# Two hybrid decoder layers on one core: attention work of both token groups moved by half a slab to four slabs, and one load moved six slabs earlier

## The chip, the cores and the metric

The kernel runs on one core of one Trainium2 chip. The metric is the device time of one execution in microseconds (us). Before the change the median of three runs is 2673.43 us (2672.96 to 2676.93). Trainium2's engines, as the profile calls them: PE (TensorE, matrix products), DVE (VectorE), ACT (ScalarE), POOL (GpSimd), SP (SyncE, which here only issues loads). Each runs its own list of instructions in the order written and waits on semaphores for the others.

## The reference

1056 token rows of width 1024 (a prompt of 1024 and 8 sample sequences of 4 rows) go through two layers, each a mixer and a ConvFFN. What matters here is the second layer's mixer D (attention over keys that an indexer picks) and its mixer C (pooling):

```python
def index_select(qi, wi, ki_all, pos_q, k_sel):
    dots = jax.nn.relu(jnp.einsum('nthd,nsd->nths', qi, ki_all))
    score = jnp.einsum('nth,nths->nts', wi, dots).astype(jnp.float32)
    admissible = jnp.arange(ki_all.shape[1])[None, :] <= pos_q[:, None]
    score = jnp.where(admissible[None], score, -jnp.inf)
    _, idx = lax.top_k(score, k_sel)      # 256 of the prompt's, 129 of a sample's 516
    return idx

def sparse_attend(q, ks, vs, idx, pos_q):
    logits = jnp.einsum('nthd,ntkhd->nthk', q, ks).astype(jnp.float32) * ATT_SCALE
    valid = (idx <= pos_q[None, :, None])[:, :, None, :]
    p = jax.nn.softmax(jnp.where(valid, logits, -jnp.inf), axis=-1).astype(q.dtype)
    return jnp.einsum('nthk,ntkhd->nthd', p, vs)

def odd_mixer(x, pool_hist, pos, attn_fn, w_in, c_w, c_scale, w_out):
    ...
    pooled = multiscale_pool(ext, pos).reshape(n, t, C_GROUPS, C_GROUP_W)
    c_out = jnp.einsum('ntgc,gcd->ntgd', pooled, c_w).reshape(n, t, C_W) * c_scale
    att = attn_fn(q, k, v, qi, ki, wi).reshape(n, t, ATT_W)
    y = jnp.concatenate([c_out, att], axis=-1) @ w_out
    return y, ext[:, -POOL_HIST:], k, v, ki

def conv_ffn(x, hist, w_up, conv_w, conv_b, w_down):
    hu = x @ w_up
    ext = jnp.concatenate([hist, hu], axis=1)
    hc = causal_dwconv(ext, conv_w) + conv_b
    y = (jax.nn.silu(hc[..., :D_FF]) * hc[..., D_FF:]) @ w_down
    return y, ext[:, -(CONV_W - 1):]
```

## The kernel before

**Slabs.** All large products are cut into 400 slabs, one weight block of 128 output columns each, numbered n in time. The tokens are in two groups: GA (the first 512 prompt rows) and GB (the other 512 and the 32 sample rows). A slab of depth 8 is 24 matmuls of 512 columns for GA and 48 of 272 for GB: each weight is split into a high part WH (copied by ACT, L1096) and a rest WL (subtracted by POOL, L1580), each input into XH and XL, and three products are added. SP loads the weights (RAW, L611) into a ring of three buffers, so the load of slab n waits until slab n-3 is multiplied. Products go to two pairs of PSUM banks in turn, so slab n also waits until slab n-2 is emptied (by ACT in up projections, by DVE, tile Z, in down projections).

**Stages that matter.** GB's first ConvFFN covers n = 150 to 209 (`F0C` to `O1A`); GA's second ConvFFN covers n = 240 to 315 (`F1A` to `O1B`), then comes GB's output projection from n = 316 (`O1B`). A ConvFFN is four blocks: 2*nb up slabs and then 8 down slabs, nb = 4, 6, 6, 6. Below, "slab +k" is slab F1A+k; +0 to +7, +16 to +27, +36 to +47 and +56 to +67 are up, the others down. In an up slab ACT empties the banks (extA or extB, cvA or cvB), DVE adds two convolution taps (L1877, L1879) and after each pair of slabs multiplies the halves; ACT and DVE split the hidden chunk (HHA, HLA). At the end of each block PE waits for the last chunk's HLA (or HL).

**Work beside the slabs.** Every engine calls `beside(n, end)` twice per slab: end = 0 in PE's middle of a slab (before ACT and DVE empty it), end = 1 after it. This is where attention runs, and fixed tables of n decide what is called where:

- Prompt attention: `units_at(n, end)` gives for each of 16 pairs of heads the half slab of each step. GA's pairs begin every 6 half slabs (`A_FIRST`, `A_PERIOD`) beside GB's first ConvFFN, GB's every 4 (`B_FIRST`, `B_PERIOD`) from slab +37. The steps are logits (PE, L927), row maximum (DVE), exp (ACT, L1353), reciprocal (DVE, L2343), scaling of the probabilities (ACT, tile PRA or PRB, L1357), turning them (PE, L941, into one PSUM bank), copying the turned ones (ACT, PTA or PTB, L1369), the product with the values (PE, L956), copy (ACT, L1378) and rest (DVE, L2349).
- GB's search: DVE's `best` units (MAX8 and MATCH_REPLACE8 on SC, L2215 and L2213) find the 256 best of blocks 4 and 5; `TOP45` says how many stand in each slab. Blocks 6 and 7 are found by bisection: `threshold` (small DVE operations on tk, one step for each `STEPS67` entry from +10) and `signs_of` (ACT, L1303, two sign passes per step) wait for each other, and `threshold` stands last in DVE's beside.
- Sample search: 16 `sample_round`s (MAX8 and MATCH_REPLACE8 on ssc, L2183 and L2185) and a `sample_bias`, all DVE.
- Sample attention: `sample_at(n)` and `kept_at(n)`, counted from F1A + `S_FIRST`: eight slabs with the logits of one sequence each (PE, L871), then eight with its values (PE, L892 and L895), with a softmax for each four sequences, PE's L904 and ACT's copies of the result (atts, L1340) at a = 12 and 16. Pages of keys and values are loaded by SP two sequences ahead.
- Mixer C of GB: the pooled rows lie in DRAM; ACT issues the load into pooledB and of cw1 (L1443, L1444), which lie over the searches' scores and biases; `c_mixed` (PE, L976), `c_kept` (ACT, L1385) and `c_rest` (DVE, L2356) follow the last slab of GA's ConvFFN, and groups 2 and 3 of `c_mixed` wait for `c_rest` of groups 0 and 1.

Of the kernel before, what the change touches and what calls it, by code (L numbers as in the profile page):

```python
# [106 lines left out]
def centred_rows(q, n, lag=0):  # L107
# [9 lines left out]
DOTS67 = 1  # L117
S_DOTS, S_FIRST = 4, 16
B_FIRST, B_PERIOD = 74, 4
TOPA = dict(zip(range(I1A + 16, F0C + 26), [2] * 32))  # L120
TOP45 = dict(zip(list(range(F1A + 2, F1A + 7)) + list(range(F1A + 16, F1A + 42)),
                 [3, 3, 2, 2, 2] + [4] * 12 + [5] * 8 + [4, 5, 5, 5, 5, 4]))
BEST = TOPK_P // 8
TOPS = (2, 3), (4,), (5,)
assert sum(TOPA.values()) == 2 * BEST and sum(TOP45.values()) == 4 * BEST

# [12 lines left out]
def units_at(n, end):  # L139


    if F0C <= n < O1A:
        p, first, begins = 2 * (n - F0C) + end, 0, [A_FIRST + A_PERIOD * r for r in range(16)]
    elif F1A <= n < O1B:
        p, first = 2 * (n - F1A) + end, 32
        begins = [B_FIRST + B_PERIOD * r for r in range(16)]
    else:
        return [[]] * 9

    def pair(lag):  # L150
        return [first + 2 * r + x for r in range(16) if begins[r] == p - lag for x in range(2)]

    return [pair(0), pair(1), pair(2), pair(3), pair(4), pair(5)[:1] + pair(6)[1:], pair(7), pair(7), pair(8)]

# [44 lines left out]
def build(nc, io):  # L199
    with ExitStack() as ctx:  # L200
# [248 lines left out]
        def pair(p, n, rows=P):  # L449

            return PS[0:rows, 2 * p:2 * p + 2, :].rearrange("p b t -> p (b t)")[:, 0:n]
# [635 lines left out]
        def _(act):  # L1087
# [299 lines left out]
            def beside(n, end):  # L1387
# [47 lines left out]
                if n == F1A + 55 and end:  # L1435
# [3 lines left out]
                    act.dma_start(Z[:, :, COL[GB]], xb_rows).then_inc(zb_in, 16)  # L1439
                if n == O1B - 1 and end:  # L1440
                    act.wait_ge(lg, 64)
                    act.wait_ge(atp, 64)
                    act.dma_start(pooledB[:, :, :], pooled_rows).then_inc(pooled_in, 16)  # L1443
                    act.dma_start(cw1[:, :, :], io["cw"]).then_inc(cw_in, 16)  # L1444
# [341 lines left out]
        def _(dve):  # L1786
# [571 lines left out]

            taken = [0]

            def beside(n, end):
# [23 lines left out]
                if (n, end) == (F1A + S_DOTS + 4, 0):  # L2385
                    blocked(lambda half, h: QBs[h // 2][half, :].rearrange("p (s r) -> p s r", s=SEQS)[
                        :, :, DEC * (h % 2):DEC * (h % 2) + DEC], QB_, qb_zero, 4, qb_set)
                r = 2 * (n - F1A - S_DOTS - 3)
                if end and 0 <= r < TOPK_S // 8:
                    sample_round(r)  # L2390
                    sample_round(r + 1)
                if (n, end) == (F1A + S_DOTS + 11, 0):
                    sample_bias()
# [190 lines left out]
```

## Time and profile before

| | before |
|---|---|
| median of three runs | 2673.43 us (2672.96 to 2676.93) |
| the profiled execution | 2667.54 us |
| its span, first to last instruction | 2665.8 us |
| PE busy | 2501.6 us, 94% |
| DVE, ACT, POOL busy | 1481.5, 1214.0, 1459.8 us |
| mean granted TensorE clock | 0.973 of full speed |

PE is busy in nearly all of the span, so what a change can give is in the 6% in which it is not, and in which work takes PE's place. The profiled execution is 5.9 us under the median; terms below are worked out against it.

### The profile page before, as it was taken

Reading aid. Unit: us, or ns where it says so; the run is one execution under the profiler, and the core shown is the slowest. Engines: PE = TensorE matmul, PEld = TensorE weight load, DVE = VectorE, ACT = ScalarE, POOL = GpSimd, SP = SyncE. Lnnn points to the kernel's source line nnn. Section 1 sums busy time; section 2 is a strip of 40 time slices with the busy share of each in tenths; the row PEclk is TensorE's granted clock in tenths of the full one; section 3 lists DMA queues with packets and bytes.
Section 4 is the critical chain, followed back from the end, with each engine's and each line's share of the span. In section 5 each row is a group of like instructions: output and inputs, shape, how many; then the busy total and the mean of one; then the engine's idle time right before and its main releaser. Section 6 shows DMA issues by size and latency. Waiting matters only on the chain.

```text
span 2665.8 us, 40768 instructions
## 1 busy us (share of the span) xinstructions
PE 2501.6 (94%) x15830; PEld 2198.1 (82%) x15830; DVE 1481.5 (56%) x2335; ACT 1214.0 (46%) x1958; POOL 1459.8 (55%) x2070
## 2 busy tenths in 40 slices
PE   8999999999999999999999987897799988999997
PEld 8999887888888788988989864666577777999997
DVE  2333576343575587643567458987954546452345
ACT  3211364343443434454543455675696725332333
POOL 3322677565676954444478777333334446655554
PEclk9999999999999999999999998999899998999998
DMA  3111222223323221222234321563113122223222
GB/s 139 41 41 49 88 90 91 95 91 99 95 64 117 80 81 65 78 66 78 66 101 143 96 91 61 184 188 95 40 56 103 56 92 95 86 76 100 84 90 82
DMA packets 97068, 235.51 MB, mean 88 GB/s; under 512 B 11434, under 2 KB 32458, under 8 KB 96490
## 3 DMA queue, kind: packets, MB, share of 16 engines
q1 hardware_dynamic: 85344, 210.95, 25.0%
q10 hardware_dynamic: 11530, 21.94, 2.3%
q8 instruction: 126, 2.06, 0.3%
q14 instruction: 68, 0.56, 0.1%
HBM read 219.40 MB, written 13.45 MB: 87 GB/s over the span
## 4 chain that ended last, share of the span: by engine, by line
PE 31%; DVE 12%; ACT 3%; POOL 3%; issue 2%; DMA 1%; ACTq 0%; DVEq 0%; POOLq 0%
PE PS L676 9%; PE PS L677 9%; PE PS L680 9%; DVE SC L2213 2%; DVE m8a L2215 2%; POOL WL L1580 1%; PE PS L956 1%; DVE cvA L1879 1%; PE PS L941 1%; PE PS L927 1%; PE PS L850 1%; DVE cvA L1877 1%; ACT signs L1303 0%; DVE ssc L2185 0%; POOL SC L1639 0%
## 5 line engine op out<-in xcount | busy, mean ns | idle before, releaser
L1580 POOL TENSOR_TENSOR WL<-RAW,WH 128x256 fp32r<-128x256 f32 x1440 | 1149.4, 829 | 1140.9 <-ACT WH L1096 1140.5
L676 PE MATMUL PS<-XH,WH 128*128 128x272 f32 (+2 forms) x3312 | 1059.2, 330 | 33.8 <-DVE XL L1976 9.9
L677 PE MATMUL PS<-XL,WH 128*128 128x272 f32 (+2 forms) x3312 | 1042.8, 326 | 0.0
L680 PE MATMUL PS<-XH,WL 128*128 128x272 f32 (+2 forms) x3312 | 873.1, 325 | 1.8 <-POOL WL L1580 1.8
L676 PEld LDWEIGHTS PS<-XH,WH 128*128 128x128 f32 x3312 | 628.3, 190 | 107.1 <-issue 56.6
L1096 ACT ACTIVATE WH<-RAW 128x1024 fp32r<-128x1024 f32 (+2 forms) x400 | 388.3, 971 | 635.8 <-DMA RAW<-in_slabs 609.8
L677 PEld LDWEIGHTS PS<-XL,WH 128*128 128x128 f32 x3312 | 628.5, 190 | 40.1 <-issue 1.0
L680 PEld LDWEIGHTS PS<-XH,WL 128*128 128x128 f32 x3312 | 559.1, 189 | 44.5 <-POOL WL L1580 2.4
L676 PE MATMUL PS<-HH,WH 128*128 128x272 f32 (+1 forms) x880 | 262.4, 313 | 13.1 <-DVE HL L1997 13.0
L677 PE MATMUL PS<-HL,WH 128*128 128x272 f32 (+1 forms) x880 | 260.2, 310 | 0.0
L680 PE MATMUL PS<-HH,WL 128*128 128x272 f32 (+1 forms) x880 | 215.7, 310 | 0.0
L1870 DVE TENSOR_SCALAR cvB<-extB,fpar 128x560 f32<-128x560 f32 x88 | 55.9, 635 | 254.4 <-POOL extB L1700 210.2
L1877 DVE SCALAR_TENSOR_TENSOR cvB<-extB,fpar,cvB 128x560 f32<-128x560 f32 (+1 forms) x132 | 118.0, 894 | 134.4 <-ACT cvB L1247 131.3
L676 PEld LDWEIGHTS PS<-HH,WH 128*128 128x128 f32 x880 | 167.0, 190 | 25.8 <-DVE HL L1997 14.1
L1924 DVE TENSOR_TENSOR Z<-Z,PS 128x512 f32<-128x512 f32 (+1 forms) x96 | 67.6, 704 | 213.4 <-PE PS L680 212.4
L677 PEld LDWEIGHTS PS<-HL,WH 128*128 128x128 f32 x880 | 166.9, 190 | 7.9
L1244 ACT ACTIVATE extB<-PS 128x240 f32<-128x240 f32 (+3 forms) x308 | 92.2, 363 | 161.0 <-PE PS L680 161.0
L680 PEld LDWEIGHTS PS<-HH,WL 128*128 128x128 f32 x880 | 145.0, 189 | 7.3
L1879 DVE SCALAR_TENSOR_TENSOR cvB<-extB,fpar,cvB 128x560 f32<-128x560 f32 (+1 forms) x132 | 116.4, 882 | 4.7
L1625 POOL TENSOR_TENSOR Z<-Z,sqb 128x512 f32<-128x512 f32 (+1 forms) x64 | 96.3, 1522 | 13.0 <-ACT sqb L1173 13.0
L676 PE MATMUL PS<-HHA,WH 128*128 128x512 f32 x176 | 76.9, 437 | 24.2 <-DVE HLA L1997 12.1
L1303 ACT ACTIVATE signs<-SC,tk 128x896 int8<-128x896 f32 (+1 forms) x62 | 73.1, 1181 | 49.1 <-DVEq L2318 49.1
(335 smaller groups left out, 3139.7 us busy)
## 6 DMA issues: line engine op xcount, KB each, us to landing
RAW<-in_slabs SPq DMA_DIRECT2D x272, 512.0 KB, 3.7
RAW<-in_slabs SPq DMA_DIRECT2D x96, 384.0 KB, 3.1
RAW<-in_slabs SPq DMA_DIRECT2D x32, 256.0 KB, 2.7
KP<-in_ck SPq DMA_DIRECT2D x16, 256.0 KB, 3.5
VP<-in_ck SPq DMA_DIRECT2D x16, 256.0 KB, 3.4
KP<-in_cv SPq DMA_DIRECT2D x16, 256.0 KB, 3.1
VP<-in_cv SPq DMA_DIRECT2D x16, 256.0 KB, 3.0
xb_rows<-spill ACTq DMA_DIRECT2D x8, 272.0 KB, 2.4
```

Of the source, the lines that this page charges most:

```text
L676: pe.matmul(o, WH[n % 3][:, k, :], hi(k)[:, c], start=first, stop=False)
L677: pe.matmul(o, WH[n % 3][:, k, :], lo(k)[:, c], start=False, stop=False)
L680: mm = pe.matmul(o, WL[n % 3][:, k, :], hi(k)[:, c], start=False, stop=last)
L1096: act.activation(WH[n % 3][:, 0:kc, :], RAW[n % 3][:, 0:kc, :], ACT.Copy).then_inc(w_hi, 1)
L1244: ins = act.activation(dst, src_, ACT.Copy)
L1303: ins = act.activation(out, SC[b], ACT.Sign, scale=tk[:, SG, x:x + 1], bias=tk[:, CAND, x:x + 1], accum_out=total)
L1580: pool.tensor_tensor(WL[n % 3][:, rows, :], RAW[n % 3][:, rows, :], WH[n % 3][:, rows, :].bitcast(F32), ALU.subtract).then_inc(w_lo, 1)
L1625: pool.tensor_tensor(z, z, LNS[q][3][:, :], ALU.subtract).then_inc(ln_sub, 1)
L1870: dve.tensor_scalar(out, row[:, 2:2 + w], taps_w[2], taps_w[3], ALU.mult, ALU.add).then_inc(tap_sem, 1)
L1877: dve.scalar_tensor_tensor(out, row[:, 0:w], taps_w[0], out, ALU.mult, ALU.add).then_inc(tap_sem, 1)
L1879: dve.scalar_tensor_tensor(out, row[:, 1:1 + w], taps_w[1], out, ALU.mult, ALU.add).then_inc(done, 1)
L1924: dve.tensor_tensor(by_bank(z, gr), by_bank(z, gr), slot(n), ALU.add).then_inc(evac_done[n % 2], 1)
```

## The change

Three edits. The first sets where group A's pairs turn their probabilities and use the values: the first head's turn goes from 5 to 6 half slabs after the pair's beginning, the second's from 6 to 7, the values (PE) and the copy (ACT) from 7 to 9, the rest (DVE) from 8 to 10. Group B keeps its numbers. The second lets ACT issue the load of the pooled rows and of the weights at slab +69 instead of +75, behind a wait for the 64th row maximum (the last reader of the space) instead of one for the 64th logits and turn. The third starts sample attention at +20 instead of +16 and the last step of the sample search at +19 instead of +15; the sixteen rounds stand two at +7, one each at +8 to +15 and two each at +16 to +18 (before: two each at +7 to +14), and twelve of `best`'s units stand one each at +10 to +15 and two each at +16 to +18 (before: four each at +16 to +18).

```diff
--- before.py
+++ after.py
@@ -115,13 +115,15 @@
 
 A_FIRST, A_PERIOD = 8, 6
 DOTS67 = 1
-S_DOTS, S_FIRST = 4, 16
+S_DOTS, S_FIRST = 4, 20
+S_ROUNDS = dict(zip(range(F1A + S_DOTS + 3, F1A + S_FIRST - 1), [2] + [1] * 8 + [2] * 3))
 B_FIRST, B_PERIOD = 74, 4
 TOPA = dict(zip(range(I1A + 16, F0C + 26), [2] * 32))
-TOP45 = dict(zip(list(range(F1A + 2, F1A + 7)) + list(range(F1A + 16, F1A + 42)),
-                 [3, 3, 2, 2, 2] + [4] * 12 + [5] * 8 + [4, 5, 5, 5, 5, 4]))
+TOP45 = dict(zip(list(range(F1A + 2, F1A + 7)) + list(range(F1A + 10, F1A + 42)),
+                 [3, 3, 2, 2, 2] + [1] * 6 + [2] * 3 + [4] * 9 + [5] * 8 + [4, 5, 5, 5, 5, 4]))
 BEST = TOPK_P // 8
 TOPS = (2, 3), (4,), (5,)
+assert sum(S_ROUNDS.values()) == TOPK_S // 8
 assert sum(TOPA.values()) == 2 * BEST and sum(TOP45.values()) == 4 * BEST
 
 
@@ -140,9 +142,9 @@
 
 
     if F0C <= n < O1A:
-        p, first, begins = 2 * (n - F0C) + end, 0, [A_FIRST + A_PERIOD * r for r in range(16)]
+        p, first, begins, x0, x1 = 2 * (n - F0C) + end, 0, [A_FIRST + A_PERIOD * r for r in range(16)], 6, 9
     elif F1A <= n < O1B:
-        p, first = 2 * (n - F1A) + end, 32
+        p, first, x0, x1 = 2 * (n - F1A) + end, 32, 5, 7
         begins = [B_FIRST + B_PERIOD * r for r in range(16)]
     else:
         return [[]] * 9
@@ -150,7 +152,8 @@
     def pair(lag):
         return [first + 2 * r + x for r in range(16) if begins[r] == p - lag for x in range(2)]
 
-    return [pair(0), pair(1), pair(2), pair(3), pair(4), pair(5)[:1] + pair(6)[1:], pair(7), pair(7), pair(8)]
+    return [pair(0), pair(1), pair(2), pair(3), pair(4), pair(x0)[:1] + pair(x0 + 1)[1:], pair(x1), pair(x1),
+            pair(x1 + 1)]
 
 
 def dots_at(n, end):
@@ -1437,9 +1440,8 @@
                     act.wait_ge(sv_turned, 2)
                     act.wait_ge(ao_lo, 20)
                     act.dma_start(Z[:, :, COL[GB]], xb_rows).then_inc(zb_in, 16)
-                if n == O1B - 1 and end:
-                    act.wait_ge(lg, 64)
-                    act.wait_ge(atp, 64)
+                if n == F1A + B_FIRST // 2 + 32 and end:
+                    act.wait_ge(amax, 64)
                     act.dma_start(pooledB[:, :, :], pooled_rows).then_inc(pooled_in, 16)
                     act.dma_start(cw1[:, :, :], io["cw"]).then_inc(cw_in, 16)
 
@@ -2356,7 +2358,7 @@
                 dve.scalar_tensor_tensor(by_bank(XL[:, g, COL[gr]], gr), wide(gr, bank), csc[:, g:g + 1],
                                          by_bank(XH[:, g, COL[gr]].bitcast(F32), gr), ALU.mult, ALU.subtract).then_inc(cevac, 1)
 
-            taken = [0]
+            taken, rounds = [0], [0]
 
             def beside(n, end):
 
@@ -2385,11 +2387,10 @@
                 if (n, end) == (F1A + S_DOTS + 4, 0):
                     blocked(lambda half, h: QBs[h // 2][half, :].rearrange("p (s r) -> p s r", s=SEQS)[
                         :, :, DEC * (h % 2):DEC * (h % 2) + DEC], QB_, qb_zero, 4, qb_set)
-                r = 2 * (n - F1A - S_DOTS - 3)
-                if end and 0 <= r < TOPK_S // 8:
-                    sample_round(r)
-                    sample_round(r + 1)
-                if (n, end) == (F1A + S_DOTS + 11, 0):
+                for u in range(S_ROUNDS.get(n, 0) if end else 0):
+                    sample_round(rounds[0])
+                    rounds[0] += 1
+                if (n, end) == (F1A + S_FIRST - 1, 0):
                     sample_bias()
                 _, now, _, taken_now, _, _, _, _, out = units_at(n, end)
                 if out:
```

In ACT's list there are 38 loads of a function table instead of 40. What the change makes of the engines' order, at three places. First PE, in group A's sixth pair (n = 168 and on); PRA_129 and PRA_130 are the scaled probabilities of its two heads, K and QA the next pair's logits. Before:

```order
L680 MATMUL PS<-XH,WL_56 128x272 x2
L941 MATMUL PS<-ident,PRA_129 128x128 x2
L676 MATMUL PS<-XH,WH_60 128x272
...
L680 MATMUL PS<-XH,WL_57 128x272 x2
L941 MATMUL PS<-ident,PRA_130 128x128 x2
L927 MATMUL PS<-K,QA__124 128x256 x2
L676 MATMUL PS<-XH,WH_60 128x272
```

And now:

```order
L683 MATMUL PS<-XH,WL_57 128x272 x2
L944 MATMUL PS<-ident,PRA_129 128x128 x2
L930 MATMUL PS<-K,QA__124 128x256 x2
L679 MATMUL PS<-XH,WH_60 128x272
...
L683 MATMUL PS<-XH,WL_57 128x272 x2
L944 MATMUL PS<-ident,PRA_130 128x128 x2
L679 MATMUL PS<-XH,WH_61 128x272
```

The first turn moved from the end of a slab to the middle of the next one, ahead of the next pair's logits, and the second from that middle to that slab's end.

Second DVE, slab +11: Z is the down product, s and ssc the sample search, m8a and SC group B's search, tk the bisection. Before:

```order
L1917 TENSOR_TENSOR Z<-XH,XL 128x512
L1921 SCALAR_TENSOR_TENSOR Z<-Z,PS 128x512
L2183 MAX s_191<-ssc 32x8
L2185 MATCH_REPLACE ssc<-s_191,ssc 32x544
L2183 MAX s_191<-ssc 32x8
L2185 MATCH_REPLACE ssc<-s_191,ssc 32x544
L2257 TENSOR_TENSOR tk<-tk 128x2
```

And now:

```order
L1919 TENSOR_TENSOR Z<-XH,XL 128x512
L1923 SCALAR_TENSOR_TENSOR Z<-Z,PS 128x512
L2185 MAX s_191<-ssc 32x8
L2187 MATCH_REPLACE ssc<-s_191,ssc 32x544
L2215 MATCH_REPLACE SC_150<-m8a,SC_150 128x640
L2259 TENSOR_TENSOR tk<-tk 128x2
```

One round less and one unit of group B's search more stand between the slab's product and the bisection's step.

Third ACT, before the end of GA's ConvFFN (WH are weights, sqa and sqb squares for the norm). Before:

```order
L1096 ACTIVATE WH_61<-RAW_55 128x1024
L1166 ACTIVATE sqb_248<-Z 128x512
L1443 DMA pooledB<-pooled_rows 128x2176
L1444 DMA cw_224<-in_cw 128x512
L1385 ACTIVATE XH<-PS,csc 128x544 x4
```

And now, six slabs earlier:

```order
L1169 ACTIVATE sqb_248<-Z 128x512
L1372 ACTIVATE PTB<-PS 128x512 x2
L1445 DMA pooledB<-pooled_rows 128x2176
L1446 DMA cw_224<-in_cw 128x512
L1372 ACTIVATE PTB_222<-PS 128x512 x2
```

The load stood directly ahead of its use; now it stands between two copies of turned probabilities.

## Rows read from the trace of the kernel before

**Rows 1.** The profile's page, part 1: busy time of each engine
```profile
PE 2501.6 (94%) x15830; PEld 2198.1 (82%) x15830; DVE 1481.5 (56%) x2335; ACT 1214.0 (46%) x1958; POOL 1459.8 (55%) x2070
```

**Rows 2.** Who waited for whom, us 958-1375: total us, times, longest
```profile
DVE cvB L1870 <- POOL extB L1700: 69.1, 20, 5.5
ACT PRA L1357 <- DVE prc L2343: 49.9, 15, 5.4
PE PS L941 <- ACT PRA L1357: 14.1, 9, 3.3
PE PS L941 <- ACT PTA L1369: 4.1, 5, 1.1
```

**Rows 3.** Windows view, us 958-1040: length, PE, PEld, DVE, ACT, POOL, clock, DMA, GB/s
```profile
958.00:1040.00 82.00, 77.33 (x597) 75.20 (x596) 63.77 (x141) 40.87 (x91) 42.18 (x90) 0.98 0.23 73
```

**Rows 4.** Timeline about us 1141: start, duration, instruction, idle before
```profile
1141.10 0.91 ACT L1357 ACTIVATE PRA<-PRA,prc 128x256 f32<-128x256 f32 x2 [5.36 <-DVE prc L2343]
1141.67 0.44 PE L941 MATMUL PS<-ident,PRA 128*128 128x128 f32 x2 [3.27 <-ACT PRA L1357]
1141.92 1.04 ACT L1096 ACTIVATE WH<-RAW 128x1024 fp32r<-128x1024 f32 x1
1145.99 0.41 PE L941 MATMUL PS<-ident,PRA 128*128 128x128 f32 x2 [0.87 <-ACT PTA L1369]
```

**Rows 5.** Timeline where group B's pooled rows come in, and two stretches' busy time
```profile
2155.75 0.40 PE L680 MATMUL PS<-HHA,WL 128*128 128x512 f32 x1
2159.16 1.02 DVE L1940 TENSOR_TENSOR zq<-zq,sqb 128x512 f32<-128x512 f32 x1
2164.78 7.00 PE L976 MATMUL PS<-pooledB,cw 128*128 128x272 f32 x16 [8.64 <-DMA cw<-in_cw]
2167.74 0.78 DVE L2356 SCALAR_TENSOR_TENSOR XL<-PS,csc,XH 128x544 fp32r<-128x544 f32 x1 [7.56 <-ACT XH L1385]
2171.42 0.49 PE L676 MATMUL PS<-XH,WH 128*128 128x272 f32 x1
...
2140.00:2150.00 10.00, 10.00 (x45) 8.08 (x44) 6.36 (x9) 3.59 (x5) 4.95 (x6) 1.00 0.35 112
2165.00:2172.00 7.00, 7.00 (x20) 4.86 (x21) 1.96 (x3) 2.32 (x4) 0.00 (x0) 0.59 0.00 0
```

**Rows 6.** DMA issues, median us to landing; last, line 611 in us 2014-2026
```profile
RAW<-in_slabs SPq DMA_DIRECT2D x96, 384.0 KB, 3.1
...
Z<-xb_rows ACTq DMA_DIRECT2D x1, 2176.0 KB, 9.2
...
pooledB<-pooled_rows ACTq DMA_DIRECT2D x1, 1088.0 KB, 7.1
...
DMA to landing us min/median/max: 3.7/4.0/4.2
```

**Rows 7.** The sample search's instructions (tile ssc); last, one of group B's search
```profile
L2183 DVE MAX8 s<-ssc x16: 707/712/717, 1649.0 to 1693.8; 32x8 f32<-32x544 f32 x16
L2185 DVE MATCH_REPLACE8 ssc<-s,ssc x16: 696/696/699, 1649.8 to 1694.7; 32x544 f32<-32x544 f32 x16
...
1736.37 0.81 DVE L2215 MAX8 m8a<-SC 128x8 f32<-128x640 f32 x1
```

**Rows 8.** Busy time in two stretches of the third ConvFFN
```profile
1661.00:1692.50 31.50, 23.04 (x73) 17.05 (x73) 29.38 (x66) 12.80 (x23) 7.83 (x12) 0.82 0.66 212
1722.50:1779.80 57.30, 57.30 (x431) 42.15 (x429) 49.55 (x96) 46.92 (x75) 23.86 (x37) 1.00 0.74 223
```

**Rows 9.** Who waited for whom, us 1661-1836; last, tile atts in 1780-1840
```profile
PE PS L676 <- DVE Z L1921: 12.6, 7, 4.1
DVE tk L2257 <- ACT signs L1303: 2.9, 1, 2.9
DVE cvA L1877 <- ACT cvA L1247: 2.7, 2, 1.4
...
  ACT XH L1429: 1.9, 1
```

## Prediction

> **What bounds the kernel.** I read the page first: PE is busy for 94% of the span [rows 1]. So I looked for the places where PE waits, by the view of waits over each stretch that the change touches, and then for what stands ahead of such a wait in the timeline.
>
> Group A's attention (us 958 to 1375): PE waited 14.1 us in 9 places for the scaled probabilities PRA before turning them, and 4.1 us in 5 places for the copy of the first head's turned ones, together 18.2 us [rows 2]. In one of them the reader sees why: ACT scales PRA at 1141.10, after 5.36 us in which it waited for DVE's reciprocal; PE starts at 1141.67 after 3.27 us idle, so it had ended its slab at 1138.40. The second turn, half a slab on, starts at 1145.99 after 0.87 us. Between the two starts lie a turn of 0.44, that wait and 3.0 us of slab: half a slab is 3.0 us [rows 4].
>
> The pooled rows: PE ends the last slab at 2156.15 and starts their product at 2164.78, 8.64 us idle for the loads; the next slab starts at 2171.42, so the gap between slabs is 15.3 us [rows 5].
>
> The sample search: in 1661 to 1692.5 (slabs +10 to +15) DVE is busy 29.4 of 31.5 us and PE 23.0. In 1722.5 to 1779.8 (the eight slabs +20 to +27, 7.2 us each) PE is busy throughout, DVE 49.6 of 57.3 [rows 8]. Over 1661 to 1836 PE waited 12.6 us for DVE's Z [rows 9]. DVE is the bound in the down slabs and not far from it in the up slabs.
>
> **Edit 1, the turns.** Nothing is added; the steps only move. PE reaches each first turn half a slab, 3.0 us, later against the engines that prepare it: a wait of 3.27 leaves 0.3, a shorter one nothing. The second turn wants ACT's copy of the first. That copy keeps its neighbours in ACT's list, and PE now has the next pair's logits as well as half a slab between the turns, so those 4.1 us should go too. That is up to 17.9 us. Is ACT late with weights by this? Its copy WH ends at 1142.96; PE wants it one slab of 6.0 us after 1138.4, at 1144.4 [rows 4]. It is not, but by little.
>
> Against the full amount: the wait for PRA is the end of a loop with a pace of its own. ACT waits for DVE's reciprocal (49.9 us in all), its next weight copy stands behind that, POOL's rests behind the copy, and DVE waits for POOL's history copies (69.1 us) [rows 2]. In 958 to 1040 DVE is busy 63.8 of 82 us [rows 3]; what PE no longer waits at the turns there it would partly wait at the block's end. I take two thirds, **12 us**. The low end is 3 (the loop sets the pace nearly everywhere), the high end 19 (all the waits, and the 2% of clock, 1.6 us, missing from those 82 [rows 3]).
>
> **Edit 2, the load.** With the wait gone PE goes straight from the slab to the product, and the next thing that is late is DVE: groups 2 and 3 wait for the rest of groups 0 and 1, and DVE is at its sums until 2160.18. A rest takes 0.78, so group 2 starts at about 2161.1 [rows 5]. The four groups took 6.64 us at a granted clock of 0.59, for the most part the lower level of 1.2 GHz [rows 5]: 1.7 a group, and I take 1.1 at the upper level, since they partly waited. Two groups end at 2163.3. Against 2171.42 that is **8 us**. If PE's idle 3 us brings the clock down to its lower level again, as 8.64 us of it did, the two groups take 2.2 more: 6 at the low end. With DVE's sums out of the way it would be 9.
>
> What could it cost? ACT issues two loads six slabs earlier, which takes it under a microsecond while PE works from weights already split. The load then shares the DMA engines with slab loads. The nearest row is the load of Z from xb_rows, twice as large and 9.2 us long: the two slab loads beside it landed in 3.7 and 4.2 us. The slab loads in question are smaller and land in 3.1 [rows 6]. A slab there has 18 matmuls, at 0.23 us each (45 in 10 us [rows 5]) 4.2 us, and two slabs pass between issue and use; I cost it at nothing. With that cover gone each of three slab loads would cost the 1.1 us between 3.1 and 4.2.
>
> Here the Trainium skill speaks against the edit. "DMA: Bandwidth & Descriptors", section "Issuing engines are not separate DMA queues", says that loads issued by different engines end up on the same 16 DMA engines and interleave. By that rule alone a load of 7.1 us could hold slab loads back by as much and take back 7 of the 8 us; by the row beside xb_rows it takes back nothing behind its cover, and 3 us without it.
>
> **Edit 3, the sample search and attention.** DVE's work is only dealt out anew. A round is 0.71 and 0.70 and a short load of a few hundredths, which I take as 1.5 us; a unit of `best` (one MAX8 or one MATCH_REPLACE8) is 0.81, and with the short load before every second one I take 0.87 [rows 7]. From Z of slab +8 to Z of slab +14 six rounds less and four units more stand in DVE's list, 5.5 us less, and there that shows in full, since DVE is the bound [rows 8]. Then it is given back: +14 and +15 carry a round and a unit each in place of two rounds at +14; +16 to +18 cost 2 x 1.5 - 2 x 0.87 = 1.3 more each, and the search's last step (three instructions like a MAX8 and two short ones, about 3 us) moves from +15 to +19. PE has no sample logits in +16 to +19 any more, so these slabs go at DVE's pace. By slab +20 DVE has done the same work as before. So the gain is not the shift but the idle time of DVE that it removes, and I count only that:
>
> - DVE waited 2.9 us for signs once [rows 9], at slab +28: ACT's copies of atts stood ahead of the signs and waited for PE, itself waiting at the block's end. After the change none stands at +28 (they are at +32, as before, and +36). 2.9 us.
> - DVE waited 2.7 us in two places for cvA [rows 9], each where ACT loads a table again behind a sample exp. The second exp now stands at +27, with no silu behind it: 1.35 us.
> - DVE waited 1.9 us for ACT's XH from atts, behind two sign passes [rows 9]. At +38 the same step stands after convolution taps and ACT is further ahead; I let 0.6 remain: 1.3 us.
>
> Sum **5.5 us**. Bounds: 7.5, all three rows, and -6 by rival C.
>
> **Sum.** 12 + 8 + 5.5 = 25.5 us. From the profiled execution 2667.54 - 25.5 = 2642.0; that execution lies 5.9 under the median of the runs, so as a median 2673.43 - 25.5 = **2648 us**.
>
> **Rivals.** What this measurement can tell from no change is about 0.2%, 5 us.
>
> *A. As forecast*, 0.54: 2637 to 2660.
>
> *B. Group A's waits move*, 0.17. The loop has its own pace, and PE, early at the turn, waits for emptied banks or for HL. For it: DVE's 69.1 us behind POOL. Against: in 958 to 1040 DVE, ACT and POOL are each busy under 80% [rows 3]. 3 + 8 + 5.5 = 16.5, **2657 us**.
>
> *C. The late sample search hurts*, 0.10. DVE reaches the search's end at +19 behind 3 x 1.3 + 3 = 6.9 us of extra work, and PE's first sample logits at +20 wait for it. For it: nothing hides DVE there. Against: 5.5 us were won just before. If these are lost again, edit 3 gives about -6: 12 + 8 - 6 = 14, **2659 us**.
>
> *D. More than counted*, 0.08: 19 + 9 + 7.5 = 35.5, **2638 us**.
>
> *E. The load collides with slab loads*, 0.04, the mechanism of the page above: 7.1 us returned, 18.4 left, **2655 us**.
>
> *F. Slower*, 0.04: value pages late in down slabs. Sequences 2 to 5 got theirs in up slabs of 7.2 us; now 2 to 7 get them in down slabs, six matmuls or 1.4 us shorter, and PE's values wait for them. A page is half a slab load; slab loads landed in 3.7 to 4.2 us [rows 6], and between issue and use lie two slabs, 11.6 us, of which issuing four pages takes the half. Six waits outweigh 25.5 us only from 4.3 us each. At 6 us each it is **2684 us**. No row shows such landings.
>
> *G. No change*, 0.03: the turns' waits all move (0), edit 3 costs 6, the load gives 6: **2673 us**.
>
> The Trainium skill's "TensorE: Matmul & The Clock Gate", section "Why this matters for your kernels", warns that idle gaps between bursts of matmuls bring the clock down; by it edit 2 gives its low end, 6 us, and the sum 23.5. The clock of 0.59 after 8.64 us idle [rows 5] agrees with the rule, and leaves open whether 3 us suffice.
>
> **How the numbers follow.** The time is rival A's. 2635 to 2662 holds A, B, C, D and E and leaves out F, G and D's tail. Faster by over 0.2% are A to E less a tail of C: 0.91. Slower is F and a little of G: 0.05. The rest is 0.04.
>
> **What would show it.** In the changed profile: PE's wait for PRA before L944 down from 14.1 to under 3 us, and no larger HL waits (B, if there are). No DMA wait before L979, and about 7 us instead of 15.3 between GA's last slab and the next. Slab +16 begun some 5 us sooner against +10, but +20 only 2 to 4; no wait of 2.9 us for signs at +28. Wrong: PE waiting long before L874 at slab +20 with DVE not ahead at +36, or L895 waiting for pages.

## The result, and the profile after

The changed kernel takes 2655.2 us (median of 6 runs, 2650.7 to 2659.35) against 2673.44 before (6 runs, 2667.97 to 2680.49): ratio 0.9936, 95% interval 0.992 to 0.9952, that is 17 us faster (13 to 21). Its profiled execution took 2654.70 us, 12.8 less than that of before. The forecast was 25.5 less and 2648, range 2635 to 2662. The time lies in the range; one of the three terms was far too large. One of the seven executions of a later kernel, edit 2 alone, took 8526 us and stands in no number below.

The page's part 1 for the changed kernel shows why totals don't help here: PE has 2.7 us less to be busy with than in [rows 1], out of 2500.

```profile
PE 2498.9 (94%) x15830; PEld 2198.8 (83%) x15830; DVE 1483.4 (56%) x2335; ACT 1209.5 (46%) x1956; POOL 1456.6 (55%) x2070
```

So I cut both executions at the slabs. The length of a stretch of slabs is the start of the first matmul of the slab behind it less that of its own first, from the timeline of PE. Stretches that no edit touches show how far this can be trusted: slabs 88 to 103 take 83.42 us in both, 292 to 303 take 92.84. Where the granted clock falls in one execution and not in the other they differ by 1 to 7 us (end of the document).

| slabs | before | after | what is there |
|---|---|---|---|
| 150 to 161 | 86.4 | 84.0 | GB's first ConvFFN, up; group A's attention to 209 |
| 162 to 169 | 47.3 | 49.3 | down |
| 170 to 181 | 88.7 | 85.3 | up |
| 182 to 189 | 43.1 | 44.1 | down |
| 190 to 201 | 91.6 | 86.3 | up |
| 202 to 209 | 38.9 | 44.7 | down |
| **150 to 209** | **396.1** | **393.8** | edit 1: -2.3 |
| 250 to 255 | 31.3 | 26.4 | +10 to +15, down |
| 256 to 259 | 30.1 | 23.9 | +16 to +19, up |
| 260 to 267 | 57.2 | 64.1 | +20 to +27, up |
| 268 to 309 | 347.7 | 345.1 | +28 to +69 |
| **250 to 309** | **466.3** | **459.5** | edit 3: -6.8 |
| **310 to 315** | **43.9** | **35.2** | edit 2: -8.7 |
| 323, the norm | 20.8 | 23.8 | no edit: lower clock, +3.0 |

**Edit 1** wins 2.4, 3.4 and 5.3 us in the three up stretches and gives back 2.0, 1.0 and 5.8 in the down stretches behind them. The waits of the changed kernel over us 955 to 1375 (total, times, longest), beside [rows 2]:

```profile
DVE cvB L1872 <- POOL extB L1702: 48.7, 17, 5.3
DVE cvB L1872 <- issue: 33.6, 9, 5.3
ACT PRA L1360 <- DVE prc L2345: 40.6, 10, 5.2
PE PS L679 <- DVE HL L1999: 8.1, 3, 4.4
PE PS L944 <- ACT PRA L1360: 7.5, 5, 2.7
PE PS L679 <- ACT WH L1099: 2.4, 2, 1.4
```

Two more lines of the view of [rows 2], the kernel before:

```profile
POOL WL L1580 <- ACT WH L1096: 213.9, 62, 6.6
DVE cvB L1870 <- issue: 19.1, 7, 4.9
```

PE's waits at the turns fell from 18.2 us to 7.5, but it now waits 8.1 us (before 2.6) for the rest of the last chunk at block ends and 2.4 for a weight copy. "Issue" stands for a wait that the profile gives no releaser. In all sixteen of these DVE starts 0.09 or 0.10 us after POOL's history copy ends, as it does where POOL is named, so they are the same wait. Together it was 88.2 us before and is 82.3 now: DVE waits for POOL nearly as long as it did. The timeline of the changed kernel about the last block end (slab 202 begins at us 1301.48) shows in which chain that rest stands (start, duration, instruction, idle before and its releaser):

```profile
1303.53 0.72 DVE L1999 TENSOR_TENSOR HL<-hfB,HH 128x544 fp32r<-128x544 f32 x1
1304.16 0.22 DVE L2345 RECIPROCAL prc<-psm 128x1 f32<-128x1 f32 x2
1304.35 1.33 ACT L1360 ACTIVATE PRA<-PRA,prc 128x512 f32<-128x512 f32 x2 [4.22 <-DVE prc L2345]
1305.59 0.83 ACT L1099 ACTIVATE WH<-RAW 128x768 fp32r<-128x768 f32 x1
1306.50 2.11 POOL L1582 TENSOR_TENSOR WL<-RAW,WH 128x256 fp32r<-128x256 f32 x3 [4.97 <-ACT WH L1099]
1308.68 0.20 POOL L1702 COPY extB<-fhist 128x16 f32<-128x16 f32 x1
1308.98 0.57 DVE L1872 TENSOR_SCALAR cvB<-extB,fpar 128x560 f32<-128x560 f32 x1 [4.41 <-POOL extB L1702]
...
1312.14 0.66 ACT L1206 ACTIVATE HH<-hfB 128x544 fp32r<-128x544 f32 x1 [3.11 <-DVE hfB L2019]
1312.83 0.72 DVE L1999 TENSOR_TENSOR HL<-hfB,HH 128x544 fp32r<-128x544 f32 x1 [0.72 <-ACT HH L1206]
```

Read it downward. DVE takes the reciprocals at 1304.16, behind its taps. ACT had waited 4.22 us for them, scales, and only then copies the weights (1305.59). POOL, 4.97 us idle for that copy, makes the weight's rest, and only behind it stands its copy of the history, done at 1308.88. DVE waited 4.41 us for it before the next taps, behind which the hidden chunk, HH and HL follow. HL ends at 1313.55, and PE, idle for 2.46 us, needs it there. Behind that wait the granted clock is 0.60 (us 1314.8 to 1319.1), and slab 203 takes 4.2 us where it takes 2.8 at full clock in a later kernel (the change with early reciprocals); so of the 5.8 us in slabs 202 to 209 some 1.4 are clock. DVE, ACT, POOL and DVE wait for each other in a ring, once per slab with a reciprocal. PE's wait at the turn was one place where this ring showed.

**Edit 2** did what it says. The changed kernel's timeline where [rows 5] has 15.3 us between the slabs:

```profile
2148.34 2.00 PE L979 MATMUL PS<-pooledB,cw 128*128 128x272 f32 x8
2151.48 1.02 DVE L1942 TENSOR_TENSOR zq<-zq,sqb 128x512 f32<-128x512 f32 x1
2152.43 1.46 DVE L2358 SCALAR_TENSOR_TENSOR XL<-PS,csc,XH 128x544 fp32r<-128x544 f32 x2
2153.34 2.07 PE L979 MATMUL PS<-pooledB,cw 128*128 128x272 f32 x8 [3.01 <-DVE XL L2358]
```

The slab's last matmul ends at 2148.50, the pooled product follows at once, and the second pair waits 3.01 us for DVE's rests behind its last sum at 2151.48. The next slab starts at 2155.05: 6.5 us between slabs (7.0 from the start of that last matmul, as an expectation below has it).

**Edit 3.** The windows view of the changed kernel: +10 to +15, +16 to +19, +20 to +27 (for the forecast's stretches see [rows 8]), and last the pooled stretch:

```profile
1660.30:1686.80 26.50, 20.61 (x73) 15.29 (x73) 24.80 (x53) 12.96 (x22) 7.99 (x11) 0.88 0.54 182
1686.80:1710.70 23.90, 23.90 (x97) 19.20 (x98) 22.14 (x44) 16.31 (x26) 12.14 (x19) 0.93 0.50 154
1710.70:1774.80 64.10, 58.59 (x330) 41.12 (x328) 57.75 (x113) 47.41 (x75) 25.25 (x39) 0.95 0.58 178
2148.00:2155.40 7.40, 4.39 (x21) 3.36 (x20) 5.32 (x7) 3.44 (x5) 4.86 (x6) 1.00 0.22 71
```

In +16 to +19 PE is busy throughout, 23.9 of 23.9 us: it does not go at DVE's pace there. DVE falls behind instead, and at +20 PE stands. The timeline there:

```profile
1718.84 0.72 DVE L2192 MAX8 s<-ssc 32x8 f32<-32x544 f32 x1
...
1721.12 0.71 DVE L2200 SCALAR_TENSOR_TENSOR sbias<-ssc,sbias 32x544 bf16<-32x544 f32 x1
1721.93 1.93 PE L874 MATMUL PS<-KP,QBs 128*32 128x512 f32 x8 [5.51 <-issue]
```

The search's last step runs from 1718.84 to 1721.83; PE's first sample logits start at 1721.93, after 5.5 us idle (0.6 before). That is rival C's wait, at rival C's place.

### The profile page after: what moved, and what is told of

Its sections match the earlier page's. It is cut to its first block, busy times and chain, and to the rows that moved or that the text cites. A ratio compares the mean times of both kernels' runs of the same rounds, so it can differ in the third digit from the quotient of the medians.

```text
span 2653.0 us, 40770 instructions
## 1 busy us (share of the span) xinstructions
PE 2498.9 (94%) x15830; PEld 2198.8 (83%) x15830; DVE 1483.4 (56%) x2335; ACT 1209.5 (46%) x1956; POOL 1456.6 (55%) x2070
## 4 chain that ended last, share of the span: by engine, by line
PE 30%; DVE 12%; ACT 3%; POOL 3%; issue 2%; DMA 0%; ACTq 0%; DVEq 0%; POOLq 0%
PE PS L679 9%; PE PS L680 9%; PE PS L683 9%; DVE SC L2215 2%; DVE m8a L2217 2%; POOL WL L1582 1%; DVE cvA L1881 1%; PE PS L959 1%; DVE cvA L1879 1%; PE PS L853 1%; PE PS L944 1%; PE PS L930 1%; POOL SC L1641 0%; DVE ssc L2187 0%; DVE HLA L1999 0%
```

## The experiments

Twelve kernels, each timed 4 to 12 times beside the kernel before. A ratio is to the kernel before, with its 95% interval; stretches are from the profiled execution, and stand for a term where the whole time is too noisy. How well they repeat: the kernels with group A untouched have 396.1 to 396.6 us in slabs 150 to 209, those with the load untouched 43.5 to 44.7 in 310 to 315, and those without any of edit 3 between 464.2 and 466.3 in 250 to 309.

| kernel | ratio (interval) | 150 to 209 | 250 to 309 | 310 to 315 |
|---|---|---|---|---|
| before | | 396.1 | 466.3 | 43.9 |
| the change | 0.9936 (0.9920 to 0.9952) | 393.8 | 459.5 | 35.2 |
| edit 1 alone | 0.9994 (0.9984 to 1.0005) | 392.2 | 466.1 | 44.1 |
| edit 2 alone | 0.9962 (0.9947 to 0.9978) | 396.4 | 466.3 | 36.8 |
| edit 3 alone | 0.9982 (0.9969 to 0.9995) | 396.3 | 459.6 | 44.0 |
| edits 2 and 3 | 0.9961 (0.9947 to 0.9976) | 396.2 | 459.8 | 35.5 |
| turns only | 1.0018 (1.0005 to 1.0032) | 400.2 | 464.2 | 44.7 |
| before + early reciprocals | 0.9951 (0.9931 to 0.9970) | 378.3 | 464.3 | 43.5 |
| change + early reciprocals | 0.9886 (0.9864 to 0.9909) | 375.0 | 461.2 | 36.6 |
| change + later scaling | 0.9887 (0.9867 to 0.9908) | 377.8 | 459.7 | 36.9 |
| attention alone 4 slabs later | 0.9997 (0.9982 to 1.0012) | 396.6 | 461.9 | 44.7 |
| change + early reciprocals, attention at +21 | 0.9899 (0.9877 to 0.9920) | 375.6 | 461.9 | 36.6 |
| change + both groups' reciprocals early, rests first | 0.9859 (0.9840 to 0.9879) | 375.0 | 458.3 | 33.3 |
| the same + later scaling | 0.9879 (0.9856 to 0.9902) | 378.3 | 457.9 | 33.3 |

### Each edit alone

The diffs are the parts of the change: for edit 1 `units_at`, for edit 2 the place and the wait of the load, for edit 3 the rest.

> Edit 1 alone (group A's turns half a slab later, its values a slab later), the load and the sample search as before. The forecast: 12 us faster than before, PE's waits for scaled probabilities and for the turned copy gone from 18 us to a few. The rival (the waits move; in the profile of the changed kernel the same stretch shows 7.5 us for the probabilities, 8.1 us for the last chunk's rest at block ends where it was 2.6, and 2.4 us for the weight copy): 2 to 3 us faster, the eight slabs at the ends of blocks at 162, 182 and 202 longer by what the slabs ahead of them are shorter.

> Edit 2 alone (the pooled rows loaded at the 64th row maximum). The forecast: 8 us faster. By the profile of the changed kernel the gap ahead of group B's output projection falls from 15.3 to 7.0 us, but the stretch of 8 slabs behind it takes 3.0 us longer, since the norm's small products at its end ran at the lower clock. If that comes with the edit, 5 to 6 us faster; if the clock falls there by chance, 8 us, and the norm's products at either clock.

> Edit 3 alone (sample search and attention stretched by four slabs). The forecast: 5.5 us faster. The changed kernel's profile has 8.0 us less between slabs 240 and 310: expected 8 if the stages don't act on each other. The rival on the other side (the late search hurts): 6 us slower.

> Edits 2 and 3 together, group A's lags as before. By the forecast 13.5 us faster than before; by the stages of the changed kernel's profile 14 us with edit 1 worth only 2 to 3: then this kernel is within 3 us of the fully changed one. If edit 1 was worth its 12, this kernel stands 12 us above it.

Edit 1 alone can't be told from no change (1.6 us of 2670 by the ratio, interval -4.3 to 1.3); its stretch is 3.9 us shorter, with 5.9 us more in slabs 202 to 209, as in the changed kernel. Edit 2 alone: 10 us faster (6 to 14), its stretch 7.1 shorter. Edit 3 alone: 4.8 us faster (1.3 to 8.3), its stretch 6.7 shorter. The ratios of the three alone add up to 16.5 us, the whole change gives 17: they don't act on each other by an amount that shows, with each of them known to 3 or 4 us. Edits 2 and 3 together give 10.4 us (6.4 to 14.2); the stretch of edit 1 says 2 to 4 us for what is left out, the two ratios 7 with intervals that overlap. The 3 us that the changed kernel lost in slab 323 did not come with edit 2 (20.8 us there, as before).

The gap of edit 2 alone shows what the changed kernel's own doesn't. The second pair of pooled products, and the clock meanwhile:

```profile
2165.21 3.48 PE L976 MATMUL PS<-pooledB,cw 128*128 128x272 f32 x8 [3.24 <-DVE XL L2355]
2165.00:2168.00 3.00, 2.79 (x6) 2.19 (x7) 0.76 (x2) 0.60 (x1) 0.00 (x0) 0.50 0.00 0
```

The clock is at 0.50, 1.2 GHz, and the pair takes 3.48 us in place of 2.07. Six kernels have this gap, with PE idle for 2.9 to 3.2 us in it. In five of them (all but the changed kernel) the second pair took 2.7 to 4.0 us, and the slabs stood 6.9 to 8.3 us apart; this is why the last column has 35.5 to 36.9 for these five and 35.2 for the changed kernel.

### Turns only

```diff
-        p, first, begins, x0, x1 = 2 * (n - F0C) + end, 0, [A_FIRST + A_PERIOD * r for r in range(16)], 6, 9
+        p, first, begins, x0, x1 = 2 * (n - F0C) + end, 0, [A_FIRST + A_PERIOD * r for r in range(16)], 6, 8
```

(against edit 1 alone)

> Edit 1 with half of its shift in the values: turns half a slab later as in edit 1, the values, copies and rests half a slab later instead of a slab. If the turns are what counts and the values' second half slab gives slack only, the stage from slab 150 to 210 is 3.9 us shorter than before as with edit 1 (3.9 alone, 2.3 in the changed kernel). If the copies of the values standing at the ends of blocks cost the 5.8 us that slabs 202 to 209 are longer, these slabs are back at 38.9 us and the stage gains about 9 us.

Neither: it is slower than before, by 4.8 us (1.3 to 8.5) and 4.1 in the stretch. Its waits there:

```profile
ACT PRA L1358 <- DVE prc L2344: 48.5, 14, 5.6
PE PS L957 <- ACT PTA L1370: 10.2, 8, 2.2
PE PS L677 <- DVE HL L1998: 6.9, 2, 4.4
PE PS L942 <- ACT PRA L1358: 4.5, 3, 2.2
```

With the values in the half slab behind the second turn PE waits 10.2 us in 8 places for the copy of the turned probabilities; the second half slab of shift is what made edit 1 no loss. And 202 to 209 stays at 46.2 us, so the copies of the values are not what is late at block ends. The wait went where PE came early, and DVE's wait for the history copies is 91.2 us ("issue" again included) where it was 88.2: what one would see of a ring that keeps its own pace.

### Opening the ring

Two edits that are one number each. DVE's reciprocals of group A in the half slab of ACT's exp, ahead of the taps:

```diff
-    return [pair(0), pair(1), pair(2), pair(3), pair(4), pair(5)[:1] + pair(6)[1:], pair(7), pair(7), pair(8)]
+    return [pair(0), pair(1), pair(2), pair(xr), pair(4), pair(5)[:1] + pair(6)[1:], pair(7), pair(7), pair(8)]
```

(xr is 2 for group A and 3 for group B)

> The kernel before with one thing changed: DVE takes group A's reciprocals one half slab earlier, in the same half slab as ACT's exp and ahead of the slab's taps, instead of behind them. Theory (a loop): ACT's scaling waits for a reciprocal that stands behind DVE's taps, these wait for POOL's history copies, these for POOL's weight rests, these for ACT's weight copy, and that stands behind the scaling. With the reciprocal ahead of the taps the loop is open: ACT's wait of 49.9 us for it falls under 15, PE's 14.1 us for scaled probabilities under 4, and the stage from slab 150 to 210 (396.1 us) shortens by 8 to 14 us. Rival (the engines' work alone sets the pace, or DVE now waits for ACT's exp instead): the stage changes by less than 3 us or grows.

> The changed kernel with group A's reciprocals one half slab earlier as well. Loop theory: the 8.1 us for the last chunk's rest at the block ends and the 5.8 us of slabs 202 to 209 go too, and the stage from 150 to 210 (393.8 us) falls by 8 us or more; the kernel is then faster than the changed one by as much. Rival: no difference, or 3 us slower where DVE waits for the exp.

On the kernel before this alone takes the stretch from 396.1 to 378.3 us, 17.8 less, more than expected; the time is 13 us less (8 to 18). Its waits in us 951 to 1331:

```profile
DVE cvB L1870 <- POOL extB L1700: 46.2, 18, 4.0
DVE cvB L1870 <- issue: 3.6, 2, 2.3
DVE prc L2343 <- ACT PRA L1353: 4.5, 9, 0.9
PE PS L676 <- DVE HL L1997: 4.4, 1, 4.4
PE PS L941 <- ACT PTA L1369: 1.7, 3, 0.9
ACT PRA L1357 <- DVE prc L2343: 1.0, 2, 0.8
```

ACT's wait for the reciprocal: 1.0 us in place of 49.9. PE's for PRA is no longer among them, and for the turned copy 1.7. DVE pays 4.5 us, waiting for the exp. DVE's wait for history copies is 49.8 us in place of 88.2. In the changed kernel the same edit takes 18.7 us from the stretch; slabs 202 to 209 are back at 38.3. Two things stay open. PE's 4.4 us for the last chunk's rest at slab 162 (2.6 before) stay with the reciprocals early, and no run says why. And ACT's exp waits for DVE's row maximum, 28.4 us before, 31.6 in the changed kernel and 24.1 here; no kernel moves that one, so whether it is a second link of the kind isn't known.

The other end of the ring, ACT's scaling half a slab later, reciprocals untouched:

```diff
-    return [pair(0), pair(1), pair(2), pair(3), pair(4), pair(x0)[:1] + pair(x0 + 1)[1:], pair(x1), pair(x1),
+    return [pair(0), pair(1), pair(2), pair(3), pair(xs), pair(x0)[:1] + pair(x0 + 1)[1:], pair(x1), pair(x1),
```

(xs is 5 for group A and 4 for group B)

> The changed kernel with ACT's scaling of group A's probabilities one half slab later (the half slab ahead of the first turn), the reciprocals where they were. It opens the loop at its other end: the scaling no longer waits for a reciprocal that stands behind the taps, so the weight copy behind it isn't held. Loop theory: ACT's wait for the reciprocal (40.6 us) falls under 10, and the stage from slab 150 to 210 (393.8 us) comes down by 10 us or more, toward the 375 of the kernel with early reciprocals. Rival (the earlier reciprocal helps only since the probabilities are ready for PE sooner): the scaled ones are now later, PE's 7.5 us of waits for them grow, and the stage is not shorter than 393.

The stretch falls from 393.8 to 377.8 us, though the scaled probabilities come later. Its waits:

```profile
DVE cvB L1874 <- POOL extB L1704: 34.3, 13, 5.0
PE PS L681 <- DVE HL L2001: 2.9, 1, 2.9
PE PS L946 <- ACT PRA L1362: 2.8, 5, 1.6
ACT PRA L1362 <- DVE prc L2347: 0.6, 1, 0.6
```

So it is not that PE gets its probabilities sooner. Either cut takes out the wait that holds ACT's weight copy, DVE's wait for history copies falls to 55.5 us here, and either cut wins 16 to 19 us. That the ring set the pace is thereby shown. With it open, edit 1 is worth 378.3 - 375.0 = 3.3 us.

### The parts of edit 3

Only the start of sample attention moved, the search and group B's units left in place:

```diff
-S_DOTS, S_FIRST = 4, 16
+S_DOTS, S_FIRST = 4, 20
```

> Half of edit 3: sample attention begins at slab +20 instead of +16, but the sixteen rounds, the search's last step and group B's units stay where they were. The forecast counted only idle time that the later attention removes (2.9 + 1.35 + 1.3 us) and put the new deal of DVE's work at nothing: then this gains 5.5 us and slabs 250 to 255 stay at 31.3 us. By the stages of the edit-3 kernel (4.5 us less in slabs +10 to +15, 6.1 less in +16 to +19, 6.7 more in +20 to +27, 2.9 less in +36 to +43): here PE's wait of 5.5 us at +20 should be gone, the 4.5 us at +10 to +15 not won, and the sum between slabs 240 and 310 about 3 to 5 us less than before.

Slabs 250 to 309: 4.4 us less, with nothing won in +10 to +15 (31.3) and no long wait at +20. Edit 3 whole wins 6.7 there. But by slab +28 the two are level: from +10 to +27 the changed kernel takes 114.5 us, this one 114.6, and the kernel before 118.6. So the new deal of the rounds, 4.9 us won in +10 to +15 and paid again at +20, comes to nothing there, as I had put it. The other 2.3 us lie in +28 to +69, where the two have the same work; kernels without edit 3 differ by as much there (345.4 to 347.7 us). The whole time shows no difference (0.9982 to 1.0012); slabs 36 to 87, which nobody touched, took 7.3 us longer in the profiled execution.

Sample attention one slab later still, on the changed kernel with early reciprocals; the search's rounds and its last step (+19) stay, by two more lines that aren't shown:

```diff
-S_DOTS, S_FIRST = 4, 20
+S_DOTS, S_FIRST = 4, 21
```

> The changed kernel with early reciprocals, and sample attention begun at +21 in place of +20, the search and its last step left where they are (+19). Theory: PE's wait of 5.5 us at +20 is for the search's last step, two slabs of loads and DVE's backlog behind it; one slab more of cover takes it off, and slabs 250 to 268 (115 us) are 3 to 5 us shorter. Rival: DVE's work is what is late, the same 5 us are waited elsewhere before +28 (at +21, or for the last chunk's rest at +28), and the stretch from 250 to 276 keeps its length within 1 us.

The rival holds. The wait at +20 is gone, and slabs 250 to 275 take 171.7 us as against 171.8: PE now waits 0.9, 2.7 and 3.5 us for ACT's convolution half (cvA) at +21, +22 and +27, and ahead of each of them ACT had waited 2.1 to 3.4 us for DVE (a threshold, hfA, a row maximum). DVE's work is what is late there.

### A faster version

In the changed kernel with early reciprocals: those of group B early too, and DVE's first two pooled rests ahead of the last sums (behind them only the other two are left, a line that isn't shown).

```diff
                         projected(n + m, m, c0 == 0, c0 == 0)
+                        if n + m == O1B - 1:
+                            c_rest(0, GB)
+                            c_rest(1, GB)
                         if c0 + nb == FC:
```

> The changed kernel with early reciprocals, and two edits in other stages, to be read there. First, group B's reciprocals one half slab earlier too: if the same loop holds in slabs 277 to 310, the 12 us and 2 us waits for rests at +41 and +43 shrink; if those waits are of work and of a bank only, slabs 276 to 310 keep their 199 us (I expect under 2 us). Second, DVE's rests of the first two pooled products stand ahead of the last norm sums: PE's 3.0 us idle between the pooled products falls to about 1, and slab 310 to 316 is 2 us shorter than 36.6.

It is the fastest of all: 2632.7 us, 38 us less than before (32 to 43). Its timeline between the pooled products:

```profile
2131.06 2.00 PE L981 MATMUL PS<-pooledB,cw 128*128 128x272 f32 x8
2133.25 1.48 DVE L2363 SCALAR_TENSOR_TENSOR XL<-PS,csc,XH 128x544 fp32r<-128x544 f32 x2 [1.30 <-ACT XH L1390]
2134.18 2.07 PE L981 MATMUL PS<-pooledB,cw 128*128 128x272 f32 x8 [1.12 <-DVE XL L2363]
2134.64 0.68 DVE L1939 TENSOR_TENSOR zs<-zs,Z 128x512 f32<-128x512 f32 x1
```

PE waits 1.12 us in place of 2.91, the sums follow behind, and 310 to 315 take 33.3 us in place of 36.6. The 3.3 us, more than the 2 expected, are that wait and the clock: the second pair takes 2.07 us, 3.54 without this edit. Slabs 276 to 309 take 287.5 us; the kernel with group A's early reciprocals has 289.5 there (the 199 of the expectation is a slip), but others with edit 3 and group B's reciprocals in their old place have 288.2 to 288.9, so group B's early ones give 1 to 2 us. The waits at +41 and +43 are 10.5 and 2.0 us (11.8 and 2.8): no ring like group A's, whose opening gave 16 to 19, bounds group B. Last, the later scaling on top:

```diff
-    return [pair(0), pair(1), pair(2), pair(xr), pair(4), pair(x0)[:1] + pair(x0 + 1)[1:], pair(x1), pair(x1),
+    return [pair(0), pair(1), pair(2), pair(xr), pair(xs), pair(x0)[:1] + pair(x0 + 1)[1:], pair(x1), pair(x1),
```

> The fastest kernel so far (the changed one with both groups' reciprocals early and the pooled rests ahead of the norm sums) with group A's scaling half a slab later as well, so that the loop is open at both ends. If either opening alone already takes the loop out of the bound, the stage from slab 150 to 210 stays at 375 us within 1 and the kernel is no faster. If what is left there (4.4 us for the last chunk's rest at slab 162) still comes from ACT's order, slabs 162 to 169 fall from 47.8 to the 45.1 us of the kernel with only the later scaling, and the kernel gains 2 to 3 us.

Slabs 162 to 169 fall from 47.8 to 46.4 us, but 150 to 161 and the other stretches grow, 378.3 in all: PE waits again, 3.2 us in seven places, for scaled probabilities. One cut is enough.

## Why the forecast was right, and where it was not

**Edit 1: the mis-sized term.** The step that failed is "I take two thirds, 12 us". Measured 2.3 in the changed kernel and 3.9 alone: the low end that I gave (3), with the mechanism of rival B, which I gave 0.17 and priced right (2657, measured 2655). The range held since it had been drawn to take in B; of the forecast's own way to 2648 the largest term did not come. I had named all the links: ACT behind the reciprocal, the weight copy behind ACT, POOL behind the copy, DVE behind POOL. Two of them stand in [rows 2], and POOL's 213.9 us for the copy stand in the same view. I called it a loop and then weighed it by DVE's busy share in [rows 3]. That was the error: in a ring of waits each engine idles while it waits for the next. Over slabs 150 to 209 of the kernel before, DVE was busy 229 of 396 us, ACT 187 and POOL 188, and the ring set the pace all the same, so [rows 3]'s shares under 80% say nothing against it. "What it no longer waits there it would partly wait at the block's end" was right, as a whole and not in part. My question whether ACT is late with weights had the answer "by little"; at two block ends it is (2.4 us).

**Edit 2: right, its low branch included.** 6.5 us between the slabs ("about 7 us" forecast), the term 7.0 to 8.7 by the kernels that have it, for 8. What is next late was DVE's sums, as said: the second pair starts 4.8 us behind the slab's end, 5.0 forecast. In the changed kernel the four products ran at full clock: the granted clock is 1.00 in 2148 to 2155.4 with 3.0 us of PE idle in it, and was 0.59 after 8.64 us [rows 5]. In the five other kernels with that gap it fell, and the second pair took 0.6 to 1.9 us longer; I had given 2.2 to that case. The Trainium skill's "TensorE: Matmul & The Clock Gate", section "Why this matters for your kernels", warns of idle gaps between bursts of matmuls, and by it edit 2 would have given its low end of 6. Five of the six traces agree that the clock falls, at a price that leaves 7.0 to 8.4 us; the changed kernel's does not. With DVE's sums out of the way I had 9 in place of 8; the faster version has 10.6. Rival E: slab loads in us 2100 to 2145 landed as before (3.1 us in the middle; the row is of the changed kernel, line 614), the pooled load in 7.2 for 7.1:

```profile
DMA to landing us min/median/max: 2.9/3.1/3.7
```

No 7 us were taken from anyone. The Trainium skill's "DMA: Bandwidth & Descriptors", section "Issuing engines are not separate DMA queues", says that such loads interleave on the same engines; whether or not these did, the landing times here show no cost of it, and the measurement decides.

**Edit 3: the size and the reasons right, the way there not.** Forecast 5.5; measured 6.8 in the changed kernel and 6.7 alone by the stretch, 4.8 by the ratio. Slab +16 comes 4.9 us sooner against +10, as said ("some 5"). But +20 comes 11.1 us sooner, not 2 to 4: slabs +16 to +19 did not go at DVE's pace, since PE can run ahead of DVE by the banks and DVE's backlog is paid at +20. Most of those 11 us are the sample logits that left and come back in the next eight slabs (6.9 us). Rival C's wait came with its 5.5 us, but behind the 4.9 won before it, so it did not cost what C said. Of the three idle times counted, DVE's waits in the changed kernel over us 1655 to 1965, and two of the same rows of the kernel before over 1661 to 1966 (the same slabs, up to +48), show:

```profile
DVE cvA L1879 <- ACT cvA L1250: 17.8, 8, 2.8
DVE tk L2259 <- ACT signs L1306: 5.2, 2, 2.6
DVE XL L2417 <- ACT XH L1432: 0.2, 1, 0.2
```

```profile
DVE cvA L1877 <- ACT cvA L1247: 19.9, 9, 3.2
DVE tk L2257 <- ACT signs L1303: 8.0, 3, 2.9
```

All three came. The wait for signs fell by 2.8 us (forecast 2.9), that for XH from 1.9 to 0.2 (1.3 forecast, 1.7 came), and of the two waits for cvA of 1.36 us at +21 and +25 the first is gone (1.35 forecast). They are gone as well where only the attention was moved, which won 4.4 us. The deal that I put at nothing gave nothing by +28.

**The sum.** 2.3 + 8.7 + 6.8 = 17.8 us by stretches, 17 by the ratio. 25.5 less the 9.7 of edit 1 is 15.8, so the rest of the error is small. The profiled execution is only 12.8 less: 3.0 us went at slab 323, where its clock fell, and 2 in small pieces elsewhere, whose cause is open. Value pages (F) were not late: in slabs +28 to +35 PE waits for none. Issuing four of them takes SP 3.6 us there, not the half of 11.6 that the forecast has.

## What to carry to other kernels

Before taking away a wait, follow its releaser back until the chain ends or closes. If it closes, removing the wait from the engine at the end only moves it to the next place where that engine meets the ring; look for the one order inside that closes it (here a reciprocal behind taps that don't need it). A ring hides as idle time on every engine in it, so measure it by its waits and never by busy shares, and add up an engine's waits at one place over all their releasers: DVE's wait for POOL seemed to fall by 20 us here, and 14.5 of them had only lost their name. And compare stretches between fixed points of the program, where an effect of 2 us in 2670 can show (slabs 150 to 209 repeat to 0.5 us here, 250 to 309 only to 2.1), while a whole execution differs by 5 us for reasons of its own.

## What the runs showed of the hardware

The same gap of PE brings the clock down in one execution and not in the next. At slab 36, behind the first norm, in code that no kernel here changes, the windows view (the third number from the right is the granted clock) has for the kernel before:

```profile
360.00:367.00 7.00, 4.35 (x40) 3.61 (x39) 4.31 (x6) 2.84 (x4) 5.59 (x9) 1.00 0.35 112
```

and for edit 1 alone:

```profile
360.00:367.00 7.00, 3.78 (x11) 2.72 (x10) 4.49 (x5) 1.30 (x2) 6.25 (x9) 0.72 0.20 64
367.00:374.00 7.00, 7.00 (x40) 6.07 (x40) 2.59 (x8) 2.69 (x5) 0.42 (x2) 0.50 0.25 75
```

At 0.50 to 0.72 of full speed, so largely at 1.2 GHz, slabs 36 to 39 took 35.4 us in place of 29.0; of the executions compared, three fell so (edit 1 alone, turns only, attention alone later) with 7.2 us more in slabs 36 to 87, the others by 0.3 less to 2.1 more. The norm in slab 323 is the same case: the clock was 0.54 in us 2209 to 2215 of the changed kernel and 1.00 in 2218 to 2224 of edit 2 alone, at the same small products:

```profile
2209.00:2215.00 6.00, 5.59 (x36) 4.95 (x36) 1.60 (x4) 0.62 (x1) 2.90 (x3) 0.54 0.14 54
```

```profile
2218.00:2224.00 6.00, 4.43 (x41) 4.00 (x39) 3.33 (x4) 1.71 (x2) 3.30 (x4) 1.00 0.47 175
```

That is 3 us that a comparison of two single executions would have charged to an edit. The gap between the pooled products is a third case: 2.9 to 3.2 us of idle PE, and the clock fell in five executions of six. With 1.12 us of idle (the two kernels with the rests first) it stayed at 1.00 in both.
